# Recurrent mixer on 64x64 diagonal blocks, both tiles through the stages together, values and bonus on GpSimd, output matrix started with its gated half

## The reference

```python
def rwkv7_recurrence(r, w, k, v, kk, a):          # 8 heads of 64, 256 steps
    def step(state, inp):                         # state: 64 x 64 for each head
        r_t, w_t, k_t, v_t, kk_t, a_t = inp
        sa = jnp.einsum('bhvk,bhk->bhv', state, -kk_t)
        state = (state * w_t[:, :, None, :]
                 + sa[..., None] * (kk_t * a_t)[:, :, None, :]
                 + v_t[..., None] * k_t[:, :, None, :])
        return state, jnp.einsum('bhvk,bhk->bhv', state, r_t)

def rwkv7_mix(p, ...):
    ...                                           # k, kk, decay, a and g from p
    y = rwkv7_recurrence(r_h, heads(decay), k_h, v_h, kk, heads(a))
    y = _standardize(y, RW_GN_EPS).reshape(B, S, RW_DIM) * gn_g + gn_b
    bonus = jnp.sum(r_h * k_h * r_k, -1, keepdims=True) * v_h
    return (y + bonus.reshape(B, S, RW_DIM)) * g

def mixer_ab(x, ...):
    p = x @ w_in
    ps = ps + (token_shift(ps) - ps) * mu         # ps: the part of p that is mixed with the row before
    ya = rwkv7_mix(ps, ...)                       # 512 columns
    yb = spatial_gating(pu, pv, ...)              # 512 columns, the gated ones
    return jnp.concatenate([ya, yb], axis=-1) @ w_out
```

## Time and profile before

| | us |
|---|---|
| median of 3 runs | 2994.54 |
| lowest, highest | 2993.69, 3005.55 |
| profiled execution | 2999.83 |
| its span | 2998.0 |
| TensorE busy | 2654.2 (89%) |
| VectorE busy | 1174.3 (39%) |
| ScalarE busy | 396.9 (13%) |
| GpSimd busy | 60.0 (2%) |

### The profile page before, as it was taken

How to read it: one execution, slowest core, us unless ns; L and a number is a source line. 1 busy time by engine, 2 the same in 40 slices (tenths; PEclk the granted TensorE clock), 3 DMA queues, 4 the chain that set the end, 5 groups by cost and what they waited for, 6 DMA issues and landing times.

```text
span 2998.0 us, 35241 instructions
## 1 busy us (share of the span) xinstructions
PE 2654.2 (89%) x14966; PEld 1646.3 (55%) x14966; DVE 1174.3 (39%) x2478; ACT 396.9 (13%) x740; POOL 60.0 (2%) x48
## 2 busy tenths in 40 slices
PE   9999999999999999999999999666667999756675
PEld 4579655994569845797468774222223666322221
DVE  2657624675167644776475203001102233100111
ACT  1400012100220003200121111000000312100000
POOL 0000000000000000000000000000000000000000
PEclk9999999999999999999998899878878999987878
DMA  8344463544535544344422365999999445999998
GB/s 317 99 155 169 155 175 118 167 169 161 175 99 169 179 149 154 105 169 174 147 78 92 141 244 203 421 421 421 421 421 369 167 156 200 413 421 421 421 421 327
DMA packets 248865, 703.55 MB, mean 235 GB/s; under 512 B 18827, under 2 KB 119689, under 8 KB 200323
## 3 DMA queue, kind: packets, MB, share of 16 engines
q1 hardware_dynamic: 247408, 699.43, 61.9%
q10 hardware_dynamic: 1299, 1.83, 0.2%
HBM read 698.33 MB, written 1.05 MB: 233 GB/s over the span
## 4 chain that ended last, share of the span: by engine, by line
PE 70%; DMA 21%; SPq 3%; DVE 3%; ACT 1%; issue 1%; DVEq 0%; ACTq 0%
PE lin L771 48%; PE sco L771 13%; PE trp L771 7%; DMA ring<-in_moe_w_down 5%; DMA ring<-in_moe_w_up 4%; DMA ring<-in_moe_w_gate 4%; DMA arena<-in_moe_w_down 2%; SPq L607 2%; DMA spare<-in_moe_w_gate 2%; PE trp L893 2%; DMA spare<-in_moe_w_down 1%; DMA arena<-in_moe_w_gate 1%; DVE arena L2491 1%; DMA x<-in_moe_w_up 1%; DMA arena<-in_moe_w_up 1%
## 5 line engine op out<-in xcount | busy, mean ns | idle before, releaser
L771 PE MATMUL lin<-ring,arena 128*128 128x512 f32 (+5 forms) x2460 | 907.3, 575 | 16.9 <-DMA ring<-in_moe_w_down 9.3
L771 PEld LDWEIGHTS lin<-ring,arena 128*128 128x128 f32 (+2 forms) x2460 | 399.2, 178 | 441.9 <-issue 426.4
L771 PE MATMUL sco<-ring,arena 128*32 128x512 f32 (+2 forms) x1380 | 301.8, 792 | 176.7 <-DMA ring<-in_moe_w_up 53.7
L771 PE MATMUL lin<-arena 128*128 128x128 f32 (+8 forms) x2800 | 389.2, 372 | 36.8 <-DMA arena<-in_moe_w_down 11.8
L771 PE MATMUL sco<-arena 128*32 128x512 f32 (+7 forms) x1632 | 311.6, 495 | 76.7 <-DMA ring<-in_moe_w_gate 26.8
L771 PEld LDWEIGHTS lin<-arena 128*128 128x128 f32 (+4 forms) x2800 | 263.5, 174 | 128.1 <-issue 106.3
L3094 DVE TENSOR_TENSOR arena<-arena,sco 128x512 f32<-128x512 f32 x16 | 11.0, 688 | 724.4 <-PE sco L771 724.4
L771 PEld LDWEIGHTS sco<-ring,arena 128*32 128x32 f32 (+1 forms) x1380 | 82.5, 147 | 340.1 <-issue 337.9
L771 PEld LDWEIGHTS sco<-arena 128*128 128x128 f32 (+4 forms) x1632 | 151.3, 172 | 193.7 <-issue 187.9
L771 PE MATMUL lin<-arena,ring 128*128 128x128 f32 (+2 forms) x1672 | 226.6, 300 | 0.0
L771 PEld LDWEIGHTS lin<-arena,ring 128*128 128x128 f32 (+1 forms) x1672 | 207.1, 187 | 14.6 <-issue 3.6
(11 more groups left out here) (313 smaller groups left out, 2103.7 us busy)
## 6 DMA issues: line engine op xcount, KB each, us to landing
ring<-in_w_gate_up SPq DMA_DIRECT2D x88, 1024.0 KB, 5.2
ring<-in_moe_w_up SPq DMA_DIRECT2D x87, 1024.0 KB, 26.9
ring<-in_moe_w_gate SPq DMA_DIRECT2D x75, 1024.0 KB, 27.0
arena<-in_moe_w_down SPq DMA_DIRECT2D x57, 1024.0 KB, 27.0
ring<-in_moe_w_down SPq DMA_DIRECT2D x53, 1024.0 KB, 27.0
ring<-in_w_down SPq DMA_DIRECT2D x44, 1024.0 KB, 6.1
arena<-in_moe_w_gate SPq DMA_DIRECT2D x40, 1024.0 KB, 23.3
arena<-in_moe_w_up SPq DMA_DIRECT2D x31, 1024.0 KB, 26.7
```

Source lines behind the costliest of these rows:

```text
L771: return nc.tensor.matmul(o, lhsT, rhs, start=start, stop=stop)
```

## The change

- The masks become 64 columns wide, one block of 64 for both chunks (`rw_compact`, `rw_levels`, `rw_turned`, `rw_eye`). The grams are taken for each chunk by itself, as 64x64 blocks by 128 columns into four PSUM banks, and VectorE masks a half tile with two operations (`mask_products`). A further 64x64 product replaces the first level's transposes. `rw_X`, `rw_XT`, `rw_T1` and `rw_BT` hold both tiles, 512 columns for each.
- Both tiles go through each stage together: turned rows and grams of both, then every level for the first and the second tile, then values, corrections, own values, WT, and after them the four steps of the state. Every product is 64x64 by 64 columns. `rwT` of the second tile, WT and the queries' product with the state lie in `spare`. The zeroing products are gone; accumulations are opened by the first product.
- `mixed_values` and two operations of `finish` (bonus times values, plus `gn_b`) move from VectorE to GpSimd (`mix_values`, `add_bonus`). In GpSimd's program they stand ahead of the two root requests of `finish`.
- The rows of the output matrix that belong to the gated columns are loaded and multiplied first. The order is: gated half of the first tile, recurrent half of the first, then the same for the second.
- The ten ring slots that were given back in the first tile's second level are given back after the third level's products (`first_values(1)`).

The core of the diff (new helpers and the loops that call them; what replaced lines of before is described above):

```diff
+    put("rw_compact", np.concatenate([within < at_column, within <= at_column] * 2, axis=1))
+    levels = [(a // s + 1 == b // s) & (b // s % 2 == 1) for a, b in ((within, at_column),) for s in (1, 2, 4, 8, 16, 32)]
+    put("rw_levels", np.concatenate(levels, axis=1))
+    put("rw_turned", (at_column + 1 == within) & (within % 2 == 1))
+    put("rw_eye", within == at_column)
...
+                def products_of_rows(t, u):
+
+                    if t:
+                        pe.wait_ge(gm_done, u + 1)
+                    await_transposes(2 if u == 0 else 0)
+                    for i in range(2):
+                        for j in range(2):
+                            for o in range(2):
+                                for e in range(2):
+                                    rows = rwT[t][parts[o], 2 * u + i, :, parts[e]]
+                                    last = mm(lin[parts[e], 2 * u + o, 256 * i + 128 * j:256 * i + 128 * j + 128], rows[:, 2 + j, :], rows[:, 0:2, :])
+                    last.then_inc(gm_full, 1)
+                    for i in range(2):
+                        for o in range(2):
+                            for e in range(2):
+                                rows = rwT[t][parts[o], 2 * u + i, :, parts[e]]
+                                last = mm(sco[parts[e], o, columns(t, 2 * u + i)], rows[:, 0, :], rows[:, 2, :])
+                    return last
+
+                def level_products(bank, stationary, moving, t):
                     for h in range(RW_HEADS):
-                        if h % 2 == 0:
-                            await_transposes(3 - h // 2)
-                        r = slice(64 * (h % 2), 64 * (h % 2) + 64)
-                        if t_gm.due():
-                            pe.wait_ge(gm_done, t_gm.value())
-                        queries = rwT[r, h // 2, 0:2, :].rearrange("p a b -> p (a b)")
-                        mm(sco[:, h % 2, 0:2 * P], rwT[r, h // 2, 2, :], queries)
-                        mm(sco[:, h % 2, 2 * P:4 * P], rwT[r, h // 2, 3, :], queries).then_inc(gm_full, 1)
-                    pe.wait_ge(gm_done, t_gm.n + 2)
+                        for e in range(2):
+                            last = mm(bank[parts[e], head(h)], stationary[parts[e], t, h, :], moving[parts[e], t, h, :])
+                    return last
+
+                def first_values(t):
+
+                    pe.wait_ge(values_mixed, t + 1)
+                    for h in range(RW_HEADS):
+                        for e in range(2):
+                            last = mm(trp[parts[e], t, head(h)], rw_G[parts[e], t, h, 3, :], p_ab[parts[e], t, 1024 + 64 * h:1088 + 64 * h],
+                                      start=h == 0, stop=False)
+                    return last
+
+                for t in range(NT):
+                    turn_rows(t)
+                    for u in range(2):
+                        last = products_of_rows(t, u)
+                last.then_inc(turned_full, 1)
+
+                for level in range(1, 6):
+                    for t in range(NT):
+                        pe.wait_ge(x_ready, NT * (level - 1) + t + 1)
+                        level_products(lin[:, t, :], rw_BT[level % 2], rw_X, t).then_inc(t1_full, 1)
+                    for t in range(NT):
+                        pe.wait_ge(t1_done, NT * (level - 1) + t + 1)
+                        pe.wait_ge(xt_ready, NT * (level - 1) + t + 1)
+                        if level < 5:
+                            level_products(sco[:, t, :], rw_XT, rw_T1, t).then_inc(x_full, 1)
+                        level_products(lin[:, 2 + t, :], rw_T1, rw_XT, t).then_inc(xt_full, 1)
...
+                for t in range(NT):
+                    for e in range(2):
+                        n = 2 * t + e
+                        if n:
+                            pe.wait_ge(state_done, n)
+                            pe.wait_ge(wt_done, t + 1)
+                            for pair in range(PAIRS):
+                                for o in range(2):
+                                    last = mm(lin[parts[e], o, columns(t, pair)], rw_WT[parts[o], t, P * pair + 64 * e:P * pair + 64 * e + 64],
+                                              rw_state[parts[o], pair, :], start=False, stop=pair == PAIRS - 1, one_group=False)
+                            last.then_inc(sa_full, 1)
+                            if n == 1:
+                                pe.wait_ge(wt_done, NT)
+                            for pair in range(PAIRS):
+                                for o in range(2):
+                                    last = mm(sco[parts[e], o, columns(t, pair)], rwT[t][parts[o], pair, 1, parts[e]], rw_state[parts[o], pair, :])
+                            last.then_inc(rs_full, 1)
...
+                        pe.wait_ge(sa_done, n + 1)
+                        if n < 3:
+                            for pair in range(PAIRS):
+                                for o in range(2):
+                                    h = 2 * pair + o
+                                    last = mm(lin[parts[o], 2 + e, columns(t, pair)], rw_b[parts[e], t, head(h)], rw_SA[parts[e], o, head(pair)],
+                                              start=False, stop=pair == PAIRS - 1, one_group=False)
+                            last.then_inc(state_full, 1)
+                        for pair in range(PAIRS):
+                            for o in range(2):
+                                h = 2 * pair + o
+                                last = mm(trp[parts[e], t, head(h)], rw_G[parts[e], t, h, 1, :], rw_SA[parts[e], o, head(pair)],
+                                          start=False, stop=h == RW_HEADS - 1)
+                    last.then_inc(y_full, 1)
...
+                assert tr_items[0] % 2 == 0
+                for t in range(NT):
+                    pe.wait_ge(y_read, t + 1)
+                    gated_columns(t)
...
+                for t in range(NT):
+                    for upper in (1, 0):
+                        if t == 0 and not upper:
+                            mixed_columns(0)
+                        elif t and not upper:
+                            mixed_columns(1, 2)
...
+            def mix_values(t):
+                lo, n = AB_VALUES
+                ps, before = p_ab[:, t, lo:lo + n], shifted_values[t]
+                pool.wait_ge(shift_loaded[3 + t], (48, 32)[t])
+                settle(nc.gpsimd.tensor_tensor(before, before, ps, ALU.subtract))
+                settle(nc.gpsimd.tensor_tensor(before, before, ring[:, mixer_slots["mu"], lo:lo + n], ALU.mult))
+                nc.gpsimd.tensor_tensor(ps, ps, before, ALU.add).then_inc(values_mixed, 1)
+
+            def add_bonus(t):
+                v = p_ab[:, t, 1024:1536].rearrange("p (h d) -> p h d", h=RW_HEADS)
+                bonus = rw_bonus[:, t, :].unsqueeze(2).to_broadcast([P, RW_HEADS, 64])
+                settle(nc.gpsimd.tensor_tensor(rw_bias[t].rearrange("p (h d) -> p h d", h=RW_HEADS), v, bonus, ALU.mult))
+                nc.gpsimd.tensor_tensor(rw_bias[t], rw_bias[t], ring[:, mixer_slots["gn"], 512:1024], ALU.add).then_inc(bias_ready, 1)
+
+            find_roots(ROOTS_FIRST // 2, 1)
+            find_roots((ROOTS_MIXER - NT) // 2, 8)
+            pool.wait_ge(tile_ready, 1)
+            for t in range(NT):
+                mix_values(t)
+            pool.wait_ge(values_mixed, NT)
+            pool.wait_ge(gm_done, 1)
+            for t in range(NT):
+                add_bonus(t)
+            find_roots(NT // 2, 8)
+            find_roots((ROOTS - ROOTS_FIRST - ROOTS_MIXER) // 2, 2)
...
+                for level in range(1, 6):
+                    if level < 5:
+                        for t in range(NT):
+                            level_block(level + 1, t)
+                    for t in range(NT):
+                        if level < 5:
+                            dve.wait_ge(x_full, NT * (level - 1) + t + 1)
+                            V.tensor_tensor(flat(rw_X, t), flat(rw_X, t), sco[:, t, :], ALU.subtract).then_inc(x_ready, 1)
+                        dve.wait_ge(xt_full, NT * (level - 1) + t + 1)
+                        V.tensor_tensor(flat(rw_XT, t), flat(rw_XT, t), lin[:, 2 + t, :], ALU.subtract).then_inc(xt_ready, 1)
...
+                update_state(0, 0)
+                update_state(0, 1)
+                read_output(0)
+                first = finish(0)
+                next(first)
+                update_state(1, 0)
+                next(first)
+                next(first)
+                next(first)
+                for _ in first:
+                    pass
+                read_output(1)
+                for _ in finish(1):
                     pass
```

More of the change, by code:

```diff
@@ L325, in build @@
         rw_square = at(5120, NT, 512)
-        rw_WT = at(RW + 12288, 4, P)
+        rw_WT, rw_rS = [spare[:, 1, 1024 * n:1024 * n + 1024].rearrange("p (t n) -> p t n", t=NT) for n in range(2)]
         rw_state = at(RW + 12800, 4, 64)
@@ new lines, in mixer_ab @@
+                for t in range(NT):
```

(42 more changed lines are left out.)

355 lines of the change are left out of this document (151 added, 204 removed).

## The result

The changed kernel takes 2951.48 us (median of 4 runs, 2950.69 to 2952.38) against 2994.55 us (2993.69 to 3005.55): a ratio of 0.9848, with a 95% interval of 0.9825 to 0.9871. It is faster by 43 us where the forecast was 24. The kernel before spreads more than the kernel after: 2993.7 to 3011.2 in fifteen timed runs, against 2949.7 to 2952.4 in nine. On another chip, where its median was 3005.28, the same change gained 54.6 us. The forecast started from 2994.5, and against that the gain is 43.

A forecast was written before the change was run, and what follows sets the result against it. It took TensorE to bound the 156.2 us stretch (over 80% of its chain of waits). Terms summed to 130.9 us, 25.3 less; with 1 us added for contention, 2994.5 - 24.3 = 2970 us, range 2952 to 2990.

The forecast's parts named there:

- Which clock: Step choosing TensorE's clock for the rewritten stretch: 0.50 (1.2 GHz) throughout, as in the state part, so 0.052 us a record.
- Turning the rows: Start of the stretch: turning the rows of both tiles, 2.4 us twice, 4.8 us.
- Grams: After the turned rows: grams on diagonal blocks with the product replacing first-level transposes, 192 records at 0.052, 10.0 us.
- VectorE's hold ahead of the levels: Between grams and levels: TensorE waits for four VectorE operations of 0.69 us plus hand-overs, 3.3 us.
- Levels and first values: Levels of both tiles plus first values: 960 records at 0.052 us, 49.9 us.
- Values, corrections, own values, WT: Products between levels and state steps: 240 records at 0.052 us, 12.5 us.
- Four state steps: Chain of four state steps after those products, with same-quarter outputs at 0.11 us each: 14.5 us.
- From the last output product to the output matrix: New wait for VectorE's read of the second tile's output, ahead of its gated columns, with a transposition group: 3.7 us.
- Output matrix: End of the stretch: 64 records at 0.43 us plus stops and transposes, 32.2 us; gated half first covers the finish.
- Rival 1: Full clock in the levels: 1392 records could drop to 0.026 us, 36 us, half of that kept: 2952 us; chance 0.08.
- Rivals 2 and 3: 2: diagonal pairs don't overlap, 0.11 us a record, 3033 us, chance 0.07; 3: GpSimd's values late, 8.5 us, 2979, chance 0.07.
- Rival 4: Gain given back: expert stage ends by its transfers alone, so its start and the end stay, 2994 us; chance 0.04.

The follow-up runs named there:

- e3: The kernel after, with the mixing of the values and the bonus moved back from GpSimd to VectorE: 2952.34 us.
- e6: The kernel after, with the recurrent half of the output matrix first again, in loads and products: 2951.08 us.
- e2: The kernel after, with all heads' level products on the upper diagonal block first, then those on the lower one: 2975.43 us.
- e1: The kernel after, with the ten ring slots given back with the last state step's outputs instead of in the third level: 2941.96 us.
- e9: The kernel after, with slots given back at the second state step's outputs and the second tile's output read before the first tile's root wait: 2934.82 us.
- e4: The kernel after, with levels 1 to 5 of the first tile done before those of the second: 2958.99 us.
- e10: The kernel after, with slots given back at the first product after the levels and the second tile's output read before the first tile's root wait: 2943.57 us.

## Why the prediction was wrong

The mechanism held and two terms had the wrong size. The step that failed is **Which clock**, "I take 0.50 throughout". In us, forecast and measured:

- Turning the rows: 4.8 and 4.8. Right.
- Grams: 10.0 and 4.8 (1543.94 to 1546.32, 1548.73 to 1551.2). The clock was 1.00, so 0.025 a record instead of 0.052.
- VectorE's hold ahead of the levels: 3.3 and 5.0. I had bounded the contention by 3 us and took 1; it was 1.3 on the path (e3: 3.67).
- Levels and first values: 49.9 and 33.3, a pause of 2.25 included. This is the mis-sized term. The first 64 records took 0.054 each, as forecast; then the clock rose and the rest took 0.029.
- Values, corrections, own values, WT: 12.5 and 10.6, 3.6 of it pauses.
- Four state steps: 14.5 and 15.1, a pause of 2.3 included. Later steps ran at 0.50, as forecast.
- From the last output product to the output matrix: 3.7 and 4.0, with the wait on VectorE where it was expected.
- Output matrix: 32.2 and 32.7. Right, but the reasoning that the gated half covers the finish explains nothing of it (e6).
- Sum: 130.9 and 110.4. Grams and levels alone make up 21.8 us of the difference of 20.5; the others nearly cancel.

What misled me was one row at 0.50: I carried the clock of the state part over to another place of the kernel. Those steps have eight output products in a row on one quarter, the levels have none. e2 shows that this can matter: the same levels, one quarter at a time, stayed at 0.50 for 34 us with TensorE busy throughout. But it doesn't settle the state steps. In e1 and e9, with the same eight products in a row, they ran at 1.00 throughout, behind levels at 1.00 and without a long pause; in the kernel after, e3, e4 and e10 all or most of them ran at 0.50, behind a pause of 2.3 to 3.6 us. The rule of the Trainium skill ("TensorE: Matmul & The Clock Gate", Part 1), which I had set aside with that row, was nearer for the levels of this kernel, and wrong for those of e2. Which of the two things, the pairing or the work ahead, decides in other kernels is not settled by these runs.

Rival 1 was given 0.08, and its figure came out by halving its 36 us because copies and VectorE "keep it from the end". They did not: no wait for ScalarE stands in the levels, and VectorE was busy 14.61 of 24 us. The full clock brought some 22 us in grams and levels, and what took part of it back were pauses that no rival named. That the time fell on rival 1's figure is luck: two errors, the halving and the missing pauses, met. Rivals 2 and 3 fell (0.029 and 0.054 a record; no wait for GpSimd). The price of rival 2, 0.11 us for a record alone on its quarter, was right (0.107 in e2 at 0.50); e2 lost 24 us and not 63, as its quarters still overlap where they change, and its clock rose after 34 us. Rival 4 fell, since everything behind the stretch moved with it.

The pauses cost 8.2 us by themselves and about 12 with the clock (e1). I could have asked for them: the prediction put the transfers beside the densest records of the program and checked only if the weights would come in time.

## What to carry to other kernels

Price a small product at both clock levels and carry both sums to the end. A clock read in one part of a kernel says little of another part, even for the same shape. Alternate small products between quarters of the array: two quarters gave twice the rate of one, and one quarter at a time also kept the clock low for 29 us longer. When a change makes an engine use up its instructions several times faster, look at what runs beside it on the transfer engines: moving one release by 19 us and one read ahead of a wait gave 16 us, while the move to GpSimd and the order of the halves gave at most 1 or 2. Moved too far, the weights come late.

## What the runs showed of the hardware

- With records of 0.029 us TensorE pauses, put to "issue", at places of the code that lie 127 or 128 records apart: 0 to 0.55 us beside idle transfer engines, 0.7 to 3.6 beside loads at 380 to 400 GB/s. Each pause of the kernel after ends 2 to 3 us after a packet of the instruction queue, and no such packet came in the 5 us from 1579 to 1584, where e1 has one. That the packets queue behind the loads is an inference from this and from e1, e9 and e10; the rows show when they move, not when they were asked for.
- 64x64 products by 64 columns, a pair on the diagonal in alternation: 0.029 us a record at 2.4 GHz, 0.054 at 1.2 GHz. Within a row on one quarter: 0.059 and 0.107.
- TensorE was busy 28.00 us of 28 at 0.50 in e2, and the clock did not rise. In e4 it stayed at 1.00 over eight gaps of 0.7 us.
- GpSimd's 128x512 operation on two inputs takes 1.04 to 1.78 us, and it stretches VectorE's operation on two inputs in SBUF beside it from 0.69 to as much as 1.76; one with an input in PSUM kept its 0.62.
